# Store waits moved to their readers, conditioning vectors loaded in the first norm, residual loaded tile by tile

## The reference, cut to what matters

```python
# first block
h = rms_norm(x, pre_norm_gain)
proj = h @ w_in                                   # 9 x 512 qkv columns, gates, RWKV columns
y = rwkv7_scan(r, decay, k, v, -kk, kk * a)       # recurrence over the 1024 tokens
...
# second block: conditioning vectors of the modulation
mod = silu(c) @ w_mod + b_mod                     # c_2 for the tokens, c_ctx_2 for the context
...
x = x + g1 * (merged @ w_out_2)                   # gated residual before the experts
x = x + g2 * expert_choice(modulate(rms(x)))      # 16 experts of 128 tokens
```

## Time and profile before

| | us |
|---|---|
| median of 3 runs (lowest, highest) | 3115.13 (3112.83, 3115.64) |
| the profiled execution, its own time | 3115.1 |
| its span from first to last instruction | 3113.3 |
| PE busy | 2753.3 (88%) |
| PEld busy | 2232.7 (72%) |
| DVE busy | 1510.2 (49%) |
| ACT busy | 1061.3 (34%) |
| POOL busy | 326.5 (10%) |
| DMA, mean rate | 115 GB/s |
| mean granted TensorE clock | 0.94 |

### The profile page before, as it was taken

How to read it: one execution, slowest core, us unless ns; L and a number is a source line. 1 busy time by engine, 2 the same in 40 slices (tenths; PEclk the granted TensorE clock), 3 DMA queues, 4 the chain that set the end, 5 groups by cost and what they waited for, 6 DMA issues and landing times. The chain is left out here.

```text
span 3113.3 us, 40246 instructions
## 1 busy us (share of the span) xinstructions
PE 2753.3 (88%) x16336; PEld 2232.7 (72%) x16336; DVE 1510.2 (49%) x2179; ACT 1061.3 (34%) x1868; POOL 326.5 (10%) x326
## 2 busy tenths in 40 slices
PE   5999989999899998992987999998999898919997
PEld 3777777777678887881865778747888776818786
DVE  3225543343455224236525131025666653599997
ACT  4214411111115215141236221114666521217775
POOL 0003500000100000000000000003111000102441
PEclk7999999999999998995988999998999999859999
DMA  6563661212311202007423122111000054249997
GB/s 166 188 210 109 183 195 50 70 54 66 115 49 45 79 17 86 21 25 218 139 82 124 34 65 88 73 49 40 1 1 1 26 180 113 109 152 348 377 377 266
DMA packets 269923, 357.40 MB, mean 115 GB/s; under 512 B 54987, under 2 KB 181987, under 8 KB 268076
## 3 DMA queue, kind: packets, MB, share of 16 engines
q1 hardware_dynamic: 225164, 208.91, 21.0%
q0 software_dynamic: 33056, 124.95, 12.3%
q10 hardware_dynamic: 11520, 20.98, 1.8%
HBM read 282.70 MB, written 76.80 MB: 115 GB/s over the span
## 5 line engine op out<-in xcount | busy, mean ns | idle before, releaser
L225 PE MATMUL ps<-h_hi,st_w_lo 128*128 128x512 f32 x880 | 364.2, 414 | 24.0 <-PEq L857 9.5
L226 PE MATMUL ps<-h_lo,st_w_hi 128*128 128x512 f32 x880 | 347.3, 395 | 0.0
L227 PE MATMUL ps<-h_hi,st_w_hi 128*128 128x512 f32 x880 | 347.2, 395 | 0.0
L222 DVE TENSOR_TENSOR ew_lo<-wraw,ew_hi 128x1024 fp32r<-128x1024 f32 x192 | 222.9, 1217 | 8.7 <-ACT ew_hi L219 8.0
L225 PEld LDWEIGHTS ps<-h_hi,st_w_lo 128*128 128x128 f32 x880 | 168.0, 191 | 76.6 <-issue 42.3
L219 ACT ACTIVATE ew_hi<-wraw 128x1024 fp32r<-128x1024 f32 x192 | 191.1, 1056 | 17.6 <-DMA wraw<-w_e_gate 6.7
L222 DVE TENSOR_TENSOR w_lo<-wraw,w_hi 128x1024 fp32r<-128x1024 f32 (+2 forms) x80 | 77.0, 976 | 243.6 <-ACT w_hi L219 243.4
L227 PEld LDWEIGHTS ps<-h_hi,st_w_hi 128*128 128x128 f32 x880 | 167.6, 190 | 36.5
L226 PEld LDWEIGHTS ps<-h_lo,st_w_hi 128*128 128x128 f32 x880 | 168.1, 191 | 32.8 <-issue 2.4
L222 DVE TENSOR_TENSOR st_w_lo<-wraw,st_w_hi 128x1024 fp32r<-128x1024 f32 x64 | 87.0, 1360 | 209.1 <-ACT st_w_hi L219 208.4
L225 PE MATMUL ps<-merged_hi,w_lo 128*128 128x512 f32 (+1 forms) x416 | 166.0, 399 | 9.8 <-DVE w_lo L222 9.8
(11 more groups left out here) (505 smaller groups left out, 6058.4 us busy)
## 6 DMA issues: line engine op xcount, KB each, us to landing
wraw<-w_in SPq DMA_DIRECT2D x98, 512.0 KB, 4.5
wraw<-w_e_gate SPq DMA_DIRECT2D x64, 512.0 KB, 11.9
wraw<-w_e_up SPq DMA_DIRECT2D x64, 512.0 KB, 11.2
wraw<-w_e_down SPq DMA_DIRECT2D x64, 512.0 KB, 12.4
mod_w<-w_mod POOLq DMA_DIRECT2D x12, 2048.0 KB, 9.6
gates<-st_zo ACTq DMA_DIRECT2D x48, 256.0 KB, 2.0
rw_in<-rw_scan POOLq DMA_DIRECT2D x8, 1280.0 KB, 6.2
mg_gates<-gates POOLq DMA_DIRECT2D x16, 512.0 KB, 5.0
```

The costliest lines, as they stand in the source:

```text
L222: return dve.tensor_tensor(dst, src, hi.bitcast(F32), ALU.subtract)
L225: pe.matmul(out, a[1], b[0], start=first, stop=False)
L226: pe.matmul(out, a[0], b[1], start=False, stop=False)
L227: return pe.matmul(out, a[0], b[0], start=False, stop=last)
```

## The change

- **Prep, end.** POOL's three waits for its stores go. They are made again at the head of the scan block as `dumped(...)`, on SP ahead of `blocks_in`, on POOL ahead of `rows_in`, on DVE ahead of its memsets. The last `masked(3, 1)` writes to `w1`, free by then, instead of `lbuf`, so it waits for POOL's fourth product and no longer for the store of `masked(3, 0)`.
- **Scan, end.** POOL's wait for the y stores moves to the head of `tiles` in the next block, and ACT's for the gate stores to the head of ACT's and DVE's queues there (`gates_stored`, through the `"first"` hook of `gemm`).
- **Conditioning vectors.** SP's three loads move into the first norm, behind the load of its seventh x tile (`head["sp"][6]`); DVE's memset of `cz` moves to the head of the norm, ACT's silu behind the split of pieces 0 and 1 at the norm's end. The three tiles now live in the outer stack.
- **Residual.** The one 4 MB load becomes eight loads of 512 KB with a semaphore each; `add` waits for the gate row once and for tile m when it first needs it.

```diff
             lbuf = sb(keep, "lbuf", [P, 2, 4, P])
+            cv = sb(keep, "cv", [P, KD, 2])
+            cz = sb(keep, "cz", [P, KD, 32])
+            bm = sb(keep, "bm", [P, 6, KD])
             scan_d = dram("rw_scan", [NT, P, 4, 5, P])
...
                         sp.dma_start(dst, src).then_inc(S("c_in"), 16)
+            def modulation_in(sp):
+                with nc.allow_non_contiguous_dma("per-channel vectors"):
+                    sp.dma_start(cv[:, :, 0], vec(A["c_2"][0])).then_inc(S("mod_in"), 16)
+                    sp.dma_start(cv[:, :, 1], vec(A["c_ctx_2"][0])).then_inc(S("mod_in"), 16)
+                    sp.dma_start(bm[:, :, :], A["b_mod_2"][0].rearrange("(s k p) -> p s k", p=P, s=6)
+                                 ).then_inc(S("mod_in"), 16)
+
             def lines_out(sp):
...
                 dve.memset(tab[32:33, :], MASKED).then_inc(S("at_tab"), 1)
+                dve.memset(cz[:, :, :], 0.0).then_inc(S("mod_zero"), 1)
                 dve.wait_ge(S("c_in"), 64)
...
                     piece_high(act, i)
+                act.wait_ge(S("mod_in"), 48)
+                act.wait_ge(S("mod_zero"), 1)
+                act.activation(cz[:, :, 0:2], cv[:, :, :], ACT.Silu).then_inc(S("mod_c"), 1)
             def first_lows(dve):
...
                    tail={"sp": first_loads, "act": first_highs, "dve": first_lows},
-                   head={"sp": {0: constants_in, 4: lines_out}, "pe": lines_on_pe, "dve": lines_on_dve})
+                   head={"sp": {0: constants_in, 4: lines_out, 6: modulation_in}, "pe": lines_on_pe, "dve": lines_on_dve})
             line_stack.close()
...
                 diff = wraw[:, 2, :]
-                cv = sb(st, "cv", [P, KD, 2])
-                cz = sb(st, "cz", [P, KD, 32])
-                bm = sb(st, "bm", [P, 6, KD])
                 mw = sb(st, "mod_w", [P, 2, KD, 512])
...
                 def _(sp):
-                    with nc.allow_non_contiguous_dma("per-channel vectors"):
-                        sp.dma_start(cv[:, :, 0], vec(A["c_2"][0])).then_inc(S("mod_in"), 16)
-                        sp.dma_start(cv[:, :, 1], vec(A["c_ctx_2"][0])).then_inc(S("mod_in"), 16)
-                        sp.dma_start(bm[:, :, :], A["b_mod_2"][0].rearrange("(s k p) -> p s k", p=P, s=6)
-                                     ).then_inc(S("mod_in"), 16)
                     for i in range(3, EDGE[0] + 4):
...
                 def _(act):
-                    act.wait_ge(S("mod_in"), 48)
-                    act.wait_ge(S("mod_zero"), 1)
-                    act.activation(cz[:, :, 0:2], cv[:, :, :], ACT.Silu).then_inc(S("mod_c"), 1)
                     piece_high(act, 2)
...
                     dve.wait_ge(S("rw_c"), 16 * len(pairs))
-                    dve.memset(cz[:, :, :], 0.0).then_inc(S("mod_zero"), 1)
                     dve.tensor_reduce(sel[:, :], ident[:, :].rearrange("p (j v) -> p v j", v=32)[:, 0:2, :], X, ALU.add
...
                 by_tile = lambda ap: ap.rearrange("p (n t) -> p n t", t=P)
+                last_masked = w1[:, :].rearrange("p (a j t) -> p a j t", a=2, j=4)
+                masked_in = lambda c, g: last_masked if (c, g) == (3, 1) else lbuf
                 block = st.enter_context(nc.Block())
...
                             at = (2 * c + par) * NT + 4 * g
-                            sp.dma_start(l_d[at:at + 4].rearrange("n s t -> s n t"), lbuf[:, par]
+                            sp.dma_start(l_d[at:at + 4].rearrange("n s t -> s n t"), masked_in(c, g)[:, par]
                                          ).then_inc(S("rw_ldump"), 16)
...
                         dve.wait_ge(S("rw_lmm"), 2 * c + g + 1)
-                        if 2 * c + g:
+                        if (c, g) == (3, 1):
+                            dve.wait_ge(S("rw_pool"), 4)
+                        elif 2 * c + g:
                             dve.wait_ge(S("rw_ldump"), 32 * (2 * c + g))
                         for par in range(2):
-                            dve.tensor_tensor(lbuf[:, par, :, :],
+                            dve.tensor_tensor(masked_in(c, g)[:, par, :, :],
                                               ps[:, 4 + par, :].rearrange("p (j t) -> p j t", t=P),
...
                         gp.dma_start(bonus_d[:, c, :], w2[:, :]).then_inc(S("rw_bonus"), 16)
-                    gp.wait_ge(S("rw_dab"), 128)
-                    gp.wait_ge(S("rw_drkv"), 192)
-                    gp.wait_ge(S("rw_bonus"), 64)
             wide.close()
...
                 flat = lambda ap: ap.rearrange("p h t -> p (h t)")
+                def dumped(eng):
+                    for name, value in (("rw_dab", 128), ("rw_drkv", 192), ("rw_bonus", 64)):
+                        eng.wait_ge(S(name), value)
+
                 START = EDGE[1] * 2 * KD
...
                                              ).then_inc(S(f"rw_ti{tt % 2}"), 16)
+                    dumped(sp)
                     blocks_in(sp, 3)
...
                         gp.dma_start(inb[:, tt % 2], scan_d[tt]).then_inc(S(f"rw_in{tt % 2}"), 16)
+                    dumped(gp)
                     for tt in range(2):
...
                                      ).then_inc(S(f"rw_stored{tt % 2}"), 16)
-                    for i in range(2):
-                        gp.wait_ge(S(f"rw_stored{i}"), 16 * NT // 2)
                 @block.tensor
...
                     gate_store(act, 2 * PIECES - 1)
-                    for i in range(2):
-                        act.wait_ge(S(f"st_out{i}"), 16 * (PIECES - RW))
                 @block.vector
...
                     piece_low(dve, EDGE[1] + 2)
+                    dumped(dve)
                     dve.memset(ti[:, :, :, :], 0.0).then_inc(S("rw_zeroed"), 1)
...
                 def tiles(gp, ev):
+                    for i in range(2):
+                        gp.wait_ge(S(f"rw_stored{i}"), 16 * NT // 2)
                     constants_in(gp)
...
                         soft(dve, Link(dve, "dve_link"), 0)
+                def gates_stored(kind, eng):
+                    if kind != "pe" and g == 0:
+                        for i in range(2):
+                            eng.wait_ge(S(f"st_out{i}"), 16 * (2 * 4 + 16))
                 at = {19: ("scores",), 20: ("exp",)}
...
                 gemm(qk_jobs + v_jobs, slots=slots, split=1 if g else 2, banks=4, bank0=4, pool=bias_in if g else tiles,
-                     side={"at": at, "pe": on_pe, "act": on_act, "dve": on_dve})
+                     side={"at": at, "pe": on_pe, "act": on_act, "dve": on_dve, "first": gates_stored})
                 ahead = pieces_of(wcols(w_in, (g + 1) * AW, (g + 2) * AW), "T") if g < 2 else []
...
                 def rows_io(gp, ev):
-                    gp.dma_start(g1r[:, :], row(res_gates_d[0])).then_inc(S("r2_in"), 16)
-                    gp.dma_start(x2[:, :, :], x1_d.rearrange("(t p) d -> p t d", p=P)).then_inc(S("r2_in"), 16)
+                    gp.dma_start(g1r[:, :], row(res_gates_d[0])).then_inc(S("r2_g"), 16)
+                    for t in range(NT):
+                        gp.dma_start(x2[:, t, :], x1_d[t * P:(t + 1) * P, :]).then_inc(S(f"r2_in{t}"), 16)
                     with nc.allow_non_contiguous_dma("per-channel vectors"):
...
                         link[0] = Link(dve, "dve_link")
-                        dve.wait_ge(S("r2_in"), 32)
+                        dve.wait_ge(S("r2_g"), 16)
+                    if i == 0:
+                        dve.wait_ge(S(f"r2_in{m}"), 16)
                     link[0](dve.tensor_tensor(prod[:, :], src, g1r[:, cols], ALU.mult))
...
```

## The result

| | before | after |
|---|---|---|
| median, us (lowest to highest) | 3113.98 (3110.8 to 3115.64), 4 runs | 3090.43 (3084.88 to 3093.53), 4 runs |
| profiled execution: its own time, span | 3115.1, 3113.3 | 3092.71, 3090.9 |
| ratio, 95% interval | | 0.9924, 0.9908 to 0.9940 |
| PE busy | 2753.3 | 2746.1 |
| mean granted clock | 0.94 | 0.941 |

The change saved 23.6 us (18.7 to 28.7) where 24.6 were forecast; 3090.43 us against 3090.5. "PE is n us ahead" means that the same matmul, counted from the first one, starts n us earlier than in the kernel before.

What follows compares the result with a forecast made beforehand. PE, busy 88% of the span, was taken as the bound, so only its idle time could pay. Savings of 8.6 + 4.7 + 1.3 + 10.0 = 24.6 us took 3115.1 to 3090.5 us, range 3085 to 3098.

Steps and rivals of the forecast that it cites:

- Conditioning, 8.6 predicted: Projection with token shift: PE's 6.35 us stall for `cz` and 2.4 us of slow clock go, less 0.1 for the barrier.
- the cover behind the stall: Projection with token shift: first `w_mod` load lands at about 58.5, PE comes at 61.6, so 3 us to spare.
- Preparation, 4.7 predicted: Barrier after the preparation: PE restarts at 407.8 instead of 411.6, 3.8 us, plus 0.9 us of clock.
- 0.1 to 0.3 behind the landing: Preparation's end: without the wait, POOL's DRAIN ends this many us after its stores land, near 407.4.
- nothing changes: Preparation's end: SP's two issues or the DRAIN end as late as now, so 4.7 us are lost: 3095.2; 10%.
- End of the scan, 1.3 predicted: Barrier after the scan: POOL's DRAIN ends near 810.9, PE restarts near 811.4 instead of 812.7; nothing counted for clock.
- Residual, 10.0 predicted: Output projection: with the residual in tiles, PE's 8.14 us stall and 1.9 us of slow clock go; bounds 5 and 10.2.
- the fourth rival: Output projection: eight loads share the DMA engines worse than one, PE stands, half of the 10 us lost: 3095.5; 8%.
- The DRAIN holds nothing: Preparation and scan ends: PE restarts near 405.6 and 809.4, 4.2 us more gain: 3086.3; 8%.
- Elements late: First norm: `bm` takes 17.9 us and lands at 39, the norm ends 7 us later: 3097.5; 12%.
- PE still waits: Output projection: with eight loads piece 4 and tile 0 come later, PE stands from 3.7 us on: 3095.5; 8%.
- the slower case: First barrier: the silu waits for elements landing at 162, pushing the barrier by 115 us: 3205; 2%.

Runs made afterwards that it cites:

- e1: The kernel before with the conditioning part alone (three loads, memset and silu moved): 0.9972 of the kernel before, 8.7 us faster (5.9 to 11.5).
- e9: The kernel before with the conditioning loads in the first norm, but the silu still behind the barrier: 0.9964, 11.2 us faster (5.3 to 16.8).
- e3: The kernel before with the preparation part alone, POOL's waits moved and the other buffer for the last masks: 0.9999 (0.9986 to 1.0012).
- e10: The changed kernel run once more as it is: 0.9938 (0.9924 to 0.9952) of the kernel before, median 3093.16 us.
- e6: The kernel before with only the other buffer for the last masks, POOL's waits kept at the preparation's end: 0.9995 (0.9983 to 1.0007).
- e5: The kernel before with only POOL's three waits moved to the head of the scan, last masks still in lbuf: 1.0004 (0.9992 to 1.0015).
- e4: The kernel before with only the waits of POOL and ACT moved from the scan's end to the next block: 0.9999 (0.9988 to 1.0009).
- e2: The kernel before with the residual part alone, eight loads: 0.9976 (0.9967 to 0.9985), 7.5 us faster (4.7 to 10.3).
- e8: The kernel before with the residual in two loads of 2 MB: 0.9969 (0.9955 to 0.9983), 9.7 us faster (5.3 to 14.0).
- e7: The changed kernel with the last y store issued by SP instead of POOL: 0.9938 (0.9917 to 0.9958) of the kernel before, median 3094.77 us.
- e11: The changed kernel with the last y store on SP, run a second time: 0.9926 (0.9908 to 0.9943) of the kernel before, median 3087.62 us.

## Why the prediction was right, point by point

- **Conditioning, 8.6 predicted, 8.7 in the profile, 8.7 (5.9 to 11.5) measured alone.** Stall and clock came as worked out (6.4 and 2.3 us), and the norm kept its length: the first barrier is 0.4 us earlier, as every matmul from the first on. `bm` landed at 27.1 against 28 assumed. One term was mis-sized: the cover behind the stall. The first `w_mod` load was given the median of all twelve, 9.6 us, and a cover of 3. Without `cz` to wait for, that first load took 11.0 us in after, 11.4 in e1 and 12.3 in e9, and the cover was 1.5, 1.0 and 0 us; in e9 0.19 us of waiting showed. The part works at the edge of its cover. The drain of 1.38 us that the Trainium skill (ScalarE: Activation LUTs, What ACT_TABLE_LOAD costs) puts beside the table load would have cost 1.4 us. The trace differs: from the start of the table load to the start of the silu it is 1.29 us, of which the load is 1.28, in after (46.41, 47.70) and in e9 (48.55, 49.85), and in after the split ahead of it ended at 46.39, so no drain stands on either side.
- **Preparation, 4.7 predicted.** PE's idle time fell by 3.9 us in after and by 3.5 in e3 and e10, 3.8 predicted; the clock gave 1.0 to 1.4, 0.9 predicted. Right in its mechanism (SP leaves the end, POOL's DRAIN is next), and e6 and e5 show which edit carries it, the buffer. The step "0.1 to 0.3 behind the landing" is 0.4 to 0.5. The DRAIN that was to be about 10 us long is 14.0, because its record begins ahead of POOL's last issues. SP's two issues took 5.9 us in after and 5.4 in e3, beyond any pair of short ones; they end 0.7 us before POOL's DRAIN in after. So the rival "nothing changes" had SP's issues right: 0.7 us more and SP would have begun to set the end. To undo the gain SP would have had to end 4.6 us later.
- **End of the scan, 1.3 predicted, 0.9 plus 0.4 to 0.6 of clock found,** in after and in e4. Two errors that cancel, which is luck: the DRAIN ends 4.1 us behind the issue (3.4 to the landing and 0.7 more), not the 3.6 that ending at 810.9 had assumed, and the clock, counted at nothing, made up for it.
- **Residual, 10.0 predicted, 8.3 + 1.8 - 0.6 = 9.5 in after, 9.6 in e2 and in e8.** In the timing of e2 alone 7.5 (4.7 to 10.3). The mechanism is right and the size is that of one execution. The prediction took PE's stall of 8.14 us from the one profile it had. Eight profiles of this study load the residual in one piece, and the stall is 4.1 to 8.1 us in them, 5.8 in the mean: the profile used has the longest. Here is the shortest, e4:

```profile
2604.32 0.79 PE L225 MATMUL ps<-w_hi,merged_lo 128*128 128x512 f32 x1 [4.08 <-DVEq L2812]
```

  The load took 26.5 us in the profile used and 22.7 to 24.9 in the seven others; why it varies stays open. The first tile landed 5.7 us behind its issue (5.4 to 5.7 in five profiles), 6.6 predicted. The rule to batch DMAs to 1 MiB or more (the Trainium skill, DMA: Bandwidth & Descriptors, Bandwidth) spoke for the fourth rival. The trace doesn't bear it out here: eight loads of 512 KB moved the 4 MB in 23.6 to 25.3 us (five profiles), two of 2 MB in 25.6 (one profile), one in 22.7 to 26.5 (eight profiles), and PE had no stall at the fourth group with eight or with two. What this kernel needed was a first part that lands before DVE is done with the split.
- **The sum.** 24.6 predicted, 23.6 measured (18.7 to 28.7). The other profiles tell how typical the two compared above are, since most of the 14 have a place either as before or as changed. The table has PE's time between the same two matmuls on either side of a place and its slow stretch (in the kernel before from 50 to 80 us, 390 to 425, 806 to 830 and 2588 to 2650). e9 counts as changed at `cz`, e8 at the output projection; e5 and e6 are left out at the preparation, e7 and e11 at the scan's end, as they are neither.

| place | as before, us | as changed, us | gain, means | predicted |
|---|---|---|---|---|
| `cz` | 29.6 to 30.5 (8 profiles) | 21.2 to 22.0 (6) | 8.6 | 8.6 |
| preparation | 33.6 to 35.5 (6) | 29.6 to 31.4 (6) | 4.7 | 4.7 |
| end of the scan | 23.6 to 24.1 (8) | 22.6 to 22.8 (4) | 1.2 | 1.3 |
| output projection | 58.0 to 61.4 (8) | 51.7 to 51.8 (6) | 7.7 | 10.0 |
| sum | | | 22.2 | 24.6 |

  Three terms hold in the mean, and the residual is worth 7.7 us, which is what e2's timing found (7.5). The sum of the places is near the 22.1 us of the three measured shares. That the whole change came within 1 us of the forecast is then in part luck. So is the closeness of the medians (3090.43 and 3090.5): the kernel before ran 1.1 us faster in the result than the 3115.1 that the forecast starts from.

  PE's lead in the profile of after is 22.5 us at the end, and it isn't monotonic: 16.4 us at 817, 20.1 at 1222, 11.5 at 2592, 21.2 behind the output projection (times of the kernel before). The swings between are slow stretches of the clock that differ from profile to profile, and a chain of small attention groups from 1400 to 1470 us. Example, windows of 240 to 256 us, first before, then e10:

```profile
240.00:256.00 16.00, 13.45 (x51) 8.94 (x51) 4.43 (x5) 6.51 (x7) 1.12 (x3) 0.89 0.33 101
```

```profile
240.00:256.00 16.00, 15.02 (x74) 11.55 (x76) 10.23 (x10) 12.01 (x12) 4.90 (x4) 1.00 0.18 55
```

  The kernel before has a slow stretch of 3.4 us in it and e10 none, though no edit is near. All eight profiles without the conditioning part have this stretch, and of the six with it e7 (0.89) and e9 have it and four don't. Where it is missing PE gains 1.7 us, on no term of the forecast; whether the conditioning part has to do with it isn't shown. At 0.50 such a stretch costs half its length. The kernel before ran between 3104.75 and 3122.26 us in the 32 runs beside e1 to e4, so a sum within 1 us of the measured one is closer than the measurement can vouch for; the range of 13 us was no wider than the runs bear out.
- **Rivals.** "The DRAIN holds nothing" is refuted by e4, e3 and e7. "Elements late", "PE still waits", and the slower case did not happen, by the rows above. The last x tile did land later behind the elements, at 29.1 instead of 26.4, with 4.3 us left before ACT's squares at 33.36. That the moved waits would hold something at the head of the next blocks did not happen in the changed kernel, because POOL's DRAIN still does their work; it did in e7, where the DRAIN no longer does.

## What to carry to other kernels

Removing a wait at a block's end gains only what the next-late engine leaves: look at every engine's DRAIN, not at the one that waits, and move the buffer or store that sets it (here the buffer was 3.2 of 3.5 us, the waits the rest). Load small vectors a stage early, in a stretch where no large load runs beside them, and split a large load so that its first user waits for the first part only. Where single parts lie within the spread of the runs, read PE's idle time in each profile and time the parts together. Before a stall goes into a sum, read it in more than one profile of the same code: this one was 8.1 us in the profile used and 5.8 in the mean of eight.

## What the runs showed of the hardware

- A DRAIN of POOL at a block's end lasts until the DMAs that POOL issued have landed, and 0.4 to 0.5 us more in the preparation (14.0 and 14.4 us above), 0.7 at the scan's end (4.07 us) and 0.1 behind loads. SP's DRAIN took 0.12 to 0.37 us with its stores under way: at the preparation's end in after it was over at 395.9, and the last mask store landed at 400.3. ACT's took 0.15 us with a gate store under way: at the scan's end in after it was over at 793.4, and the store landed at 796.1. A store issued by POOL before a barrier therefore costs its landing there; one issued by SP costs only its issue, 0.6 us for the y store in e7, but 5.9 for the two mask stores in after.
- With a wait on the same store ahead of it the DRAIN still takes 0.88 us more at the preparation and 1.36 at the scan's end: the wait was not free even where it ended when the store landed.
- 6144 single elements landed in 7.2 to 7.7 us in the norm, with the load of one x tile behind them (six profiles), and in 17.7 to 18.4 beside `w_mod`'s 2 MB loads (eight). SP's next issue, the eighth x tile, took 3.2 to 3.7 us behind them, against 0.33 in the kernel before.
- PE's stall for one 4 MB load was 4.1 to 8.1 us in eight profiles of the same code at this place, with the load landing in 22.7 to 26.5 us; with eight loads of 512 KB or two of 2 MB there was none.
- The slow stretches of the clock far from any edit differ between executions of the same code, and one (near 1000 us) came with a change 200 us ahead of it; its cause is open.
